# A two-layer diffusion trunk on one core: context query slices loaded sooner, rows of the expert stream placed elsewhere

## What is computed

```python
for l in range(DEPTH):                          # 2 layers
    hc, hs = modulate(xc, ...), modulate(xs, ...)
    # even layer: gated depthwise convolution + attention; odd layer: 2-D Fourier mix + short gated convolution
    xc = xc + mc[:, :, 2] * mixer(hc);  xs = xs + ms[:, :, 2] * mixer(hs)
    hc, hs = modulate(xc, ...), modulate(xs, ...)
    xc = xc + mc[:, :, 5] * peer(hc, wq, keys, u_tab, v_tab)
    xs = xs + ms[:, :, 5] * peer(hs, wq, keys, u_tab, v_tab)

def peer(xb):                                   # a block of 128 tokens
    q = xb @ wq                                 # 1024 x 2048, 8 heads of two halves
    s = q . keys                                # 8 heads x 2 halves x 128 keys
    eidx, gate = 16 best of the 16 x 16 sums of the best 16 of each half
    ue = u_tab[eidx]; act = gelu(ue . xb)       # 128 experts per token
    return sum over experts of gate * act * v_tab[eidx]
```

## Time and profile before

| what | value |
|---|---|
| median of 3 runs | 4327.29 us (4326.15 to 4329.38) |
| the profiled execution: its time, its span | 4318.79 us, 4317.0 us |
| DVE busy | 2683.9 us (62%) |
| POOL busy | 2437.2 us (56%) |
| PE busy | 2194.0 us (51%) |
| mean over the span, DMA | 366 GB/s |

### The profile page before, as it was taken

The page is one execution under the profiler, slowest core; times in us unless marked ns, Lnnn a source line. Parts: engine busy times, 40 slices in busy tenths (PEclk is TensorE's granted clock), DMA queues, the critical chain, the costliest instruction groups (busy, mean ns, idle before and its releaser), DMA issues.

```text
span 4317.0 us, 39635 instructions
## 1 busy us (share of the span) xinstructions
PE 2194.0 (51%) x11309; PEld 1043.1 (24%) x11309; DVE 2683.9 (62%) x6848; ACT 1078.3 (25%) x3593; POOL 2437.2 (56%) x2564
## 2 busy tenths in 40 slices
PE   6668656666943333334543687436933333333334
PEld 4545344334510000003430235104510000000000
DVE  3546865886657676765457554556467666666762
ACT  1232223322332222221232222322332222222221
POOL 0134534545567776774457543664477776777774
PEclk8778778678965555556775798657966555565565
DMA  9677999899999999999999989999999999999997
GB/s 296 197 283 278 350 333 353 302 363 335 397 366 409 409 409 409 409 405 355 331 398 408 358 315 347 378 408 339 358 388 409 409 408 400 405 406 398 408 406 292
DMA packets 576516, 1578.52 MB, mean 366 GB/s; under 512 B 49843, under 2 KB 237187, under 8 KB 576168
## 3 DMA queue, kind: packets, MB, share of 16 engines
q0 software_dynamic: 368640, 1342.34, 80.0%
q1 hardware_dynamic: 183570, 212.74, 14.5%
q10 hardware_dynamic: 24086, 20.92, 1.4%
HBM read 1549.63 MB, written 26.18 MB: 365 GB/s over the span
## 4 chain that ended last, share of the span: by engine, by line
DMA 31%; PE 25%; DVE 16%; POOL 12%; issue 11%; ACT 3%; SPq 3%; POOLq 0%; ACTq 0%; DVEq 0%
DMA v_ring<-in_peer_v_dram,idx_v 16%; PE ps_box L1040 10%; PE ps_v L954 7%; POOL v_ring L893 7%; DMA u_ring<-in_peer_u_dram,idx 6%; DVE u_ring L1747 5%; POOL u_ring L883 4%; DMA w_slots<-in_peer_keys_dram 3%; PE ps_box L1193 2%; DMA w_slots<-in_w_out_odd_dram 2%; DVE HT L2002 2%; DMA w_slots<-in_w_in_odd_dram 1%; SPq L455 1%; SPq L457 1%; PE ps_box L990 1%
## 5 line engine op out<-in xcount | busy, mean ns | idle before, releaser
L1747 DVE CUSTOM_DVE_ANT_0 u_ring<-u_ring,h_cur 128x1024 f32<-128x1024 f32 x1280 | 1533.3, 1217 | 664.2 <-DMA u_ring<-in_peer_u_dram,idx 646.2
L883 POOL DMA_INDIRECT u_ring<-in_peer_u_dram,idx x1280 | 1215.9, 950 | 1111.0 <-DVE act_v L1747 582.9
L954 PE MATMUL ps_v<-v_ring,w_diag 128*32 128x512 f32 x5120 | 1009.5, 930 | 1575.6 <-DMA v_ring<-in_peer_v_dram,idx_v 1406.3
L893 POOL DMA_INDIRECT v_ring<-in_peer_v_dram,idx_v x1280 | 1221.0, 954 | 749.3 <-PE ps_v L954 376.4
L954 PEld LDWEIGHTS ps_v<-v_ring,w_diag 128*32 128x32 f32 x5120 | 189.3, 146 | 2322.9 <-issue 1683.1
L1040 PE MATMUL ps_box<-HT,w_slots 128*128 128x128 f32 (+2 forms) x1728 | 472.9, 436 | 63.4 <-DMA w_slots<-in_w_in_odd_dram 32.7
L1325 ACT ACTIVATE w_v<-w_tok 32x4 f32<-32x4 f32 x1280 | 265.5, 207 | 787.8 <-DVE w_tok L1805 757.3
L1040 PEld LDWEIGHTS ps_box<-HT,w_slots 128*128 128x128 f32 x1728 | 291.1, 212 | 248.9 <-issue 153.3
L1335 ACT ACTIVATE idx_v<-idx 32x4 uint32<-32x4 uint32 x1280 | 265.5, 207 | 243.1 <-PE ps_v L954 221.0
L1341 ACT ACT_TABLE_LOAD x79 | 101.4, 1283 | 350.5 <-DVE act_v L1747 345.1
L1756 DVE TENSOR_TENSOR w_diag<-w_v,eye 128x128 f32<-128x128 f32 x320 | 92.2, 288 | 139.2 <-ACT w_v L1325 123.0
(11 more groups left out here) (191 smaller groups left out, 2189.6 us busy)
## 6 DMA issues: line engine op xcount, KB each, us to landing
w_slots<-in_peer_wq_dram SPq DMA_DIRECT2D x48, 1024.0 KB, 16.2
w_slots<-in_w_mod_dram SPq DMA_DIRECT2D x34, 1024.0 KB, 12.3
u_ring<-in_peer_u_dram,idx POOLq DMA_INDIRECT x1280, 12.2
v_ring<-in_peer_v_dram,idx_v POOLq DMA_INDIRECT x1280, 12.1
w_slots<-in_w_in_odd_dram SPq DMA_DIRECT2D x16, 1024.0 KB, 16.4
w_slots<-in_w_out_odd_dram SPq DMA_DIRECT2D x12, 1024.0 KB, 21.7
v_ring<-in_w_mod_dram SPq DMA_DIRECT2D x11, 1024.0 KB, 12.0
s_buf<-sc ACTq DMA_DIRECT2D x78, 128.0 KB
```

The lines of the kernel that those rows point to most:

```text
L883: pool.indirect_dma_start(out=u_ring[:, k % NU, :], out_offset=None, in_=u_rows, in_offset=bass.IndirectOffsetOnAxis(ap=idx[:, h % 2, k:k ...
L893: pool.indirect_dma_start(out=v_ring[:, k % NV, :], out_offset=None, in_=v_rows, in_offset=bass.IndirectOffsetOnAxis(ap=idx_v[:, h % 2, k: ...
L954: last = nc.tensor.matmul(ps_v[QUARTER * q:QUARTER * q + QUARTER, 512 * half:512 * half + 512], w_diag[:, c % GROUPS, q, :], v_ring[:, (r ...
L1747: nc.vector.tensor_tensor_reduce(u_ring[:, k % NU, :], u_ring[:, k % NU, :], h_cur[:, :], 1.0, 0.0, ALU.mult, ALU.add, act_v[:, h % 2, k:k ...
```

## The change

Four things are done.

1. **Context wq slices.** The keys of layer 0 come in one transfer of 1 MB into half of `seg_bufs`, and the eight wq slices of the context get seven slots (0 to 6, the last slice slot 0 again): slices 0 to 3 are issued ahead of the wait for the modulation, 4 to 6 ahead of the wait for the mixed x, 7 behind the store of h. PE waits for the keys once more. POOL waits for slice 6's projection before the first v gather, since four slices lie in the v ring. `load_seg(0)` goes behind the last key transpose, the sample's inputs ahead of it.
2. **Rows of segment 0.** Eight rows come ahead of the sample's norm; vg 5 to 6 after each of four steps, attend of block 0 3 to 2 after each of eight heads, conv_norm 4 to 2. ACT does its part of the first 16 rows ahead of the score slices 4 to 7, not behind.
3. **Slices ahead of two stores.** `odd_in(CTX)` and `wout_in(1, SMP, 1)` issue their first three slices before `store_seg` and `load_seg`.
4. **Rows of segment 5.** Rate cv 4 to 8, ff 1 to 2.

```diff
+WQ_SLOTS = (0, 1, 2, 3, 4, 5, 6, 0)
-RATES = {(0, SMP): {"norm": 1, "vg": 5, "vg_end": 2, "qkv": 5, "attend": (3, 3, 3, 3), "conv_norm": (4, 4), "out": (1, 2),
+RATES = {(0, SMP): {"norm": 1, "vg": 6, "vg_end": 2, "qkv": 5, "attend": (2, 3, 3, 3), "conv_norm": (2, 4), "out": (1, 2),
-         (1, SMP): {"early": 4, "norm": 1, "f": 2, "f_end": 4, "cv": 4, "cv_end": 4, "Y": 1, "ff": 1, "out": (1, 2),
+         (1, SMP): {"early": 4, "norm": 1, "f": 2, "f_end": 4, "cv": 8, "cv_end": 4, "Y": 1, "ff": 2, "out": (1, 2),
+EARLY_ROWS = 8
...
+            if key[1:3] == (0, CTX):
+                at = 2 * P * key[4]
+                return seg_bufs[:, 2:4, :].rearrange("p n d -> p (n d)")[:, at:at + 2 * P].rearrange("p (j d) -> p j d", j=2)
...
+            def wq_first(first, end):
+                for s in range(first, end):
+                    load_weight(sp, ("wq", 0, CTX, 0, s), T["peer_wq"][0], s * WC)
...
+            sp.dma_start(seg_bufs[:, 2:4, :].rearrange("p n d -> p (n d)").rearrange("p (j d) -> p j d", d=P),
+                         T["peer_keys"][0].rearrange("h j k d -> k (h j) d")).then_inc(S("keys_in"), 16)
             rows_out(1, 3, 6)
             rows_out(0, 0, 2)
+            wq_first(0, 4)
             sp.wait_ge(S("kv_out"), 32)
             sp.wait_ge(S("mod_out", 0), 96)
             load_bc(0, CTX, 4, 0, "bc_ffn")
             load_bc(0, CTX, 3, 1, "bc_ffn")
+            wq_first(4, 7)
             out_end(0, CTX, 0)
-            prep(0, CTX, 0)
+            sp.wait_ge(S("h2_tok", 0, CTX), 1)
+            sp.dma_start(hs[0], h2_tile(0, CTX, 0)).then_inc(S("hs_out", 0, CTX), 16)
+            wq_first(7, 8)
+            sp.wait_ge(S("hs_out", 0, CTX), 16)
+            sp.wait_ge(S("xa_out", 0, CTX), 16)
+            load_h(0)
 
             mix_in(0, SMP)
             prep_end(0, CTX, 0)
+            box, use = boxes[("kyT", 0, CTX, 0, 7)]
+            sp.wait_ge(box_ready[box], use + 1)
+            load_seg(0, 0, CTX)
...
             mix_in(1, CTX)
-            store_seg(3, 0)
-            load_seg(4, 0, SMP)
-            odd_in(CTX)
+            odd_in(CTX, lambda: (store_seg(3, 0), load_seg(4, 0, SMP)))
...
-            store_seg(5, 1)
-            load_seg(6, 1, SMP)
-            out_in(1, SMP, 1)
+            wout_in(1, SMP, 1, lambda: (store_seg(5, 1), load_seg(6, 1, SMP)))
+            out_end(1, SMP, 1)
...
+                    if isinstance(i, int) and (i, c) == (1, 2):
+                        box, use = boxes[("q", 0, CTX, 0, 13)]
+                        pool.wait_ge(box_ready[box], use + 1)
...
             scores(0, CTX, 0, 2, 8)
-            rows(TOPK)
+            rows(TOPK + EARLY_ROWS)
...
             third(0, 0, CTX)
+            rows(TOPK)
             scores(0, CTX, 0, 4, 8)
-            rows(TOPK)
+            rows(EARLY_ROWS)
```

More of the change, by code:

```diff
@@ L185, in mix @@
             for s in range(8):
-                order.append((("wq", l, g, q, s), ("q", l, g, q, 2 * s + 1), 2))
+                order.append((("wq", l, g, q, s), ("q", l, g, q, 2 * s + 1), 1 if (l, g) == (0, CTX) else 2))
     mix(0, CTX)
@@ L192, in plan_weights @@
     plan, counts, user = {}, [0] * NWA, [None] * NWA
-    early = len(FIRST_ORDER) + 4
+    first = len(FIRST_ORDER) + 4
     for n, entry in enumerate(order):
         key, last, dmas = entry
-        slot = n % NWA if n < early else (n - early) % NW
+        if n < first:
+            slot = n % NWA
+        elif n < first + 8:
+            slot = WQ_SLOTS[n - first]
+        else:
+            slot = (n - first - 8) % NW
         counts[slot] += 16 * dmas
@@ L709, in odd_in, with wout_in @@
                 sp.dma_start(dft_t(g), T["dft_ctx" if g == CTX else "dft_smp"]).then_inc(S("dft_in", g), 16)
-            def wout_in(l, g, q):
+            def wout_in(l, g, q, beside=lambda: None):
                 for s in range(4):
+                    if s == NW:
+                        beside()
                     load_weight(sp, ("wout", l, g, q, s), T["w_out_even" if l == 0 else "w_out_odd"][0], s * WC)
@@ L744, in prep @@
                         sp.wait_ge(S("xa_out", l, g), 16 * hi)
[L745 to L748, removed]
+                        if g == SMP:
                             load_h(5 * l + 1 + q)
@@ L1203, in scores @@
                     w = weight(pe, ("wq", l, g, q, s))
+                    if (l, g) == (0, CTX):
+                        pe.wait_ge(S("keys_in"), 16)
                     kr = weight_keys(("wq", l, g, q, s))
```

## The result

The changed kernel takes 4286.39 us (median of 6 runs, 4277.81 to 4293.91); the kernel before, run beside it, takes 4326.72 us. The ratio is 0.9912 (95% interval 0.9890 to 0.9935), so 38 us faster, 28 to 48. A second measurement, among the experiments, gave 0.9922 (0.9910 to 0.9935), 34 us. The profiled execution took 4293.91 us, the longest of its six, with a span of 4292.1 us.

The account below looks back on a forecast made before the run. The bound was taken to change by stage: transfers at 409 GB/s where only rows run, chains of waits beside mixers. 0 + 10 + 11 + 22 = 43 us off 4318.79 gave 4276, as a median 4284, range 4256 to 4312.

Parts of the forecast that it names:

- Context slices, 0 forecast: Start of segment 0: loading slices and keys in a transfer hole costs nothing and wins 0, between 3 won and 4 lost.
- Eight rows ahead of the norm, free: Ahead of the sample's norm: eight rows take 9.7 us of DVE, fit its 19.88 us idle, and are free.
- vg steps, 20 lost: Projections of segment 0: two more diagonal waits, two more groups and a topk lose 20 us, bounds 0 and 45.
- Attend 16 won: Attend of block 0: eight rows and one topk fewer on DVE's path win 16 us, bounds 8 and 19.3.
- Segment 0 in all, 0 forecast: All of segment 0: its terms sum to +1, called 0, between 18 us lost and 20 won.
- Slices of segment 4, 10 won: First projection of segment 4's mixer: a 19.32 us weight wait goes, 7.7 us is paid earlier; 10 us won.
- Slices of the last mix_out, 11 won: Last mix_out: a 20.82 us wait for its first slice goes, 7.7 us is paid earlier; 11 us won.
- Segment 5, 22 won: Twenty rows leave segment 5's end, saving 51.2 us, less 24 in four stretches and 5 for a topk; bounds 39, -10.
- the start gains too: Rival, segment 0: the eight free rows are a net gain of 20 us if vg steps hide their waits; 4264, chance 0.2.
- Segment 5 gives nothing: Rival, segment 5: moved rows win nothing as a stretch is full and rows push PE; 21 us remain, 4306, chance 0.17.
- the slices do not come sooner: Rival, slices ahead of two stores: SP is held by another wait, so 22 us won in all, 4305; chance 0.03.
- The vg steps stretch much more: Rival, segment 0's projections: at half clock behind new waits they take 56 us more, 4340, slower; chance 0.1.

Follow-up runs that it names:

- e_vg5: The changed kernel with vg 5 in place of 6 and conv_norm 4 in place of 2 in segment 0, run twice: 4282.57 us, then 4287.65 us.
- e_start: The kernel before with only the context slices, keys and row moves of segment 0, ACT's order included: 4331.21 us, ratio 1.0010.
- e_ff1: The changed kernel with segment 0's rows and ACT's order as before, and ff 1 in place of 2 in segment 5: 4287.43 us, ratio 0.9912.
- e_cv4: The changed kernel with segment 0's rows and ACT's order as before, and cv 4 in place of 8 in segment 5: 4294.59 us, ratio 0.9917.

## Why the prediction was right, step by step

The time forecast, 4284, is 2 us from the median of 4286.39. That it is so near is luck: 43 us were forecast, 38 and 34 measured, and several of its steps were wrong and made up for each other.

- *Context slices, 0 forecast:* **7 won** (3 to 12). The step failed where it counted one wait for keys and said that "the others are for topk, for ACT and for the stores of the scores, which stay". The waits for the stores got shorter, as no slices are in their way: 2.0 us, beside 1.8 for the keys. 5 of the 7 show ahead of the first projection. What the rest is was not measured.
- *Eight rows ahead of the norm, free:* **11.6 lost** ahead of the first projection (third column of the table against the second). DVE's idle time was read, and not what ACT, PE and the transfers have to do for the same rows. The norm does begin about when it did, 264.02 - 185.03 = 79.0 us behind the first key transposes, as before (261.15 - 182.17); but only as the slices' gain made up for the last store of the scores, which lands later beside the gathers. And "the first projection, 20 us after the norm's start" comes 25.9 us after it, for ACT's spread of the weights and PE's group, to which the step gave no time.
- *vg steps, 20 lost:* **20.0**, with the four waits at the four groups that were named. e_vg5 gave half of it back by taking two of them away.
- *Attend 16 won:* **11.3**, within its bounds of 8 and 19.3. *Conv_norm and cut, 5 won:* 2.8 and 0.6. *Topk after row 95, 8 lost:* 12.4. *Topk after row 111, 8 won:* 12.6. The steps before attend, left out of the sum, won 2.9. From the first projection to block 1's first score the rows lose 2.8 where the forecast was 0: right. (All these against the first column.)
- *Segment 0 in all, 0 forecast:* with the slices 4 lost (e_start), within 18 lost to 20 won.
- *Slices of segment 4, 10 won:* **5**. The waits at the next slices took 7, not 2, and three slices cost 9.0 us in the full stretch, not 7.7. *Slices of the last mix_out, 11 won:* **10**; nothing came back there, and the price was 8.6.
- *Segment 5, 22 won:* **23** by the medians, 20 by the stages. The terms were off, and their errors nearly cancel: from before to after, fT0 to cv1 grew by 2.1 us (2 forecast), fT2 to gb1 by 5.6 (9, and 5 for a topk), cv2 to gb3 by 13.5 (5), Y and ff by 9.9 (8), 31.1 in all where 29 were forecast. And the step charged the last stretch to the wrong rows. By it the sixteen cv rows win 41 - 16 - 5 = 20 and the four ff rows 10.2 - 8 = 2; the runs gave 10 to 14 for each. The stages show why:

| stage of segment 5, by PE's rows | neither (5 kernels) | cv rows alone (e_ff1) | ff rows alone (e_cv4) | both (7) |
|---|---|---|---|---|
| fT0 to gb3 | 141.5 to 141.9 | 163.5 | 141.5 | 162.7 to 165.1 |
| Y and ff | 40.9 | 49.0 | 41.9 | 50.0 to 50.8 |
| mix_out to the second norm's transposes | 29.3 to 31.3 | 26.1 | 37.6 | 33.2 to 35.0 |
| these to the last score slice | 68.1 to 75.8 | 77.4 | 65.4 | 64.2 to 67.7 |
| to the store, where the early slices are paid there | 176.5 (1) | 135.8 | 165.8 | 124.9 to 126.2 (6) |

The cv rows add 22 us to the projections, as forecast (21), but 8 more to Y and ff, where the step gave them nothing: 41 - 22 - 8 = 11, and 10.2 were measured. In Y a group waits for its v tile, as in no kernel without them; here in e_ff1:

```profile
2603.34 3.64 PE L980 MATMUL ps_v<-v_ring,w_diag 128*32 128x512 f32 x16 [5.05 <-DMA v_ring<-in_peer_v_dram,idx_v]
```

The ff rows add 1 us to Y and ff where 8 were forecast, so nearly all of their 10.2 is won. What else they do, some 7 us more ahead of the second norm and, with DVE's wait for ACT gone, some 8 less in the scores, nearly cancels in e_cv4; no row of the prediction shows that wait.

PE's timelines of before and after, cv2 to Y, show the stretch that grew most: 2578.10 - 2532.46 = 45.6 us, and 2614.80 - 2555.69 = 59.1.

```profile
2532.46 28.07 PE L1040 MATMUL ps_box<-HT,w_slots 128*128 128x512 f32 x64
...
2578.10 5.45 PE L1164 MATMUL ps_box<-dft_ch,AR 128*128 128x256 f32 x24
```

```profile
2555.69 14.35 PE L1066 MATMUL ps_box<-HT,w_slots 128*128 128x512 f32 x32
2572.91 3.13 PE L980 MATMUL ps_v<-v_ring,w_diag 128*32 128x512 f32 x16 [2.88 <-DVE w_diag L1785]
...
2611.52 3.35 PE L980 MATMUL ps_v<-v_ring,w_diag 128*32 128x512 f32 x16 [3.27 <-DVE w_diag L1785]
2614.80 5.45 PE L1190 MATMUL ps_box<-dft_ch,AR 128*128 128x256 f32 x24
```

Four groups stand here where two stood. Two of them wait for a diagonal, 2.88 and 3.27 us, and take 3.13 and 3.35 us behind it in place of 1.92: 3.13 + 3.35 + 2 x 1.92 + 6.15 - 2 x 1.92 = 12.6 us more, where two groups of 2 and one short wait were charged.

Of the rivals, "the start gains too" was half true: its slices gain, its rows do not. "Segment 5 gives nothing" and "the slices do not come sooner" are out. "The vg steps stretch much more" is out: their products take 14.0 to 14.9 us behind the waits. The Trainium skill, "TensorE: Matmul & The Clock Gate", Part 1, has the rule that an idle array falls to half its clock. The trace agrees in kind, but it cost little: the groups behind idle times of 3 to 13 us took 2.76 to 3.64 us where others take 1.92.

## What to carry to other kernels

A row moved into an engine's idle time brings its work on every engine with it; before calling it free, list what ACT, PE and the transfers do for it and what then waits for them. Where engines run hand-interleaved programs, four rows more or less can decide whether a short instruction waits behind another engine's program, and such a wait (9.3 us here) can weigh about as much as the bytes of the rows moved (10.2). And a small gain of a whole change can hide a loss in one of its parts: run alone, each part shows its own sign, and leaving the losing one out may beat the whole.

## What the runs showed of the hardware

- Three 1 MB slices put into a stretch at 409 GB/s cost 9.0 us in nine kernels, 3.0 us each or 350 GB/s, where a row of the same size costs 2.56. Why a slice costs more than a row was not tried.
- A 128 KB store lands in 1.7 us when the transfers stand nearly still, in 4.8 to 6.6 beside the gathers of rows (nine runs), and in 7.0 to 7.9 with 1 MB loads under way in another queue as well (five).
- Kernels that are the same up to the first context key transposes reach them at 182.2 to 186.8 us, and segment 1 took 445 to 454 us in kernels that do the same in it. Differences of 5 us in one profile say nothing; those between stages do.
